# Splitting layer 0's sixteen input weight halves into high and low parts, with seven slots for the unsplit halves that follow

## The reference

```python
h = rms_norm(x, norm_g)
a_u, a_v, a_g, b_q, b_k, b_v, b_g, m_q, m_g = split_cols(h @ w_in, EVEN_SPLITS)   # w_in 1024 x 4096
y_a = chunked_sgu(gelu(a_u), gelu(a_v), ...) * silu(a_g)
q = rope(rms_norm(b_q.reshape(..., 8, 2, 32)));  k likewise       # 16 sub-heads of width 32
o_b = rms_norm(diff_attention(q, k, v, lam)) ; y_b = o_b * silu(b_g)
y_m = memory_attention(m_q, mem_n, m_wkv, ...) * silu(m_g)        # keys and values from mem
return x + concat([y_a, y_b, y_m]) @ w_out
```

## Time and profile before

| what | us |
|---|---|
| median of 3 runs (1028.76 to 1029.42) | 1029.19 |
| the profiled execution | 1031.47 |
| its span, first to last instruction | 1029.7 |
| PE busy in the span | 946.3 |
| DVE busy | 445.9 |
| POOL busy | 440.5 |
| ACT busy | 328.3 |
| mean granted TensorE clock | 0.961 of full speed |

### The profile page before, as it was taken

How to read it: one execution, slowest core, us unless ns; L and a number is a source line. 1 busy time by engine, 2 the same in 40 slices (tenths; PEclk the granted TensorE clock), 3 DMA queues, 4 the chain that set the end, 5 groups by cost and what they waited for, 6 DMA issues and landing times.

```text
span 1029.7 us, 14942 instructions
## 1 busy us (share of the span) xinstructions
PE 946.3 (92%) x5860; PEld 849.2 (82%) x5860; DVE 445.9 (43%) x948; ACT 328.3 (32%) x607; POOL 440.5 (43%) x561
## 2 busy tenths in 40 slices
PE   4999899999999897989898999889999898999995
PEld 4888788888888775768798998789898898998994
DVE  1453555511357799661498126701020434322133
ACT  2201343102000144331344475444020443443441
POOL 0040000100110100002399678898270398999992
PEclk9999989999999988889899999989999999999999
DMA  8443223243434400141164435353534155555551
GB/s 340 135 163 123 82 82 102 67 159 123 162 124 164 164 6 37 41 169 50 44 246 142 143 123 187 111 173 102 204 124 164 42 179 167 177 194 181 177 181 55
DMA packets 37637, 139.33 MB, mean 135 GB/s; under 512 B 4288, under 2 KB 4288, under 8 KB 37312
## 3 DMA queue, kind: packets, MB, share of 16 engines
q1 hardware_dynamic: 37424, 136.97, 39.0%
q10 hardware_dynamic: 144, 1.41, 0.3%
HBM read 137.32 MB, written 1.05 MB: 134 GB/s over the span
## 4 chain that ended last, share of the span: by engine, by line
PE 24%; POOL 22%; DVE 2%; ACT 1%; issue 1%; DVEq 0%; ACTq 0%; POOLq 0%
POOL w_lo L1993 22%; PE psum L488 7%; PE psum L489 6%; PE psum L490 5%; PE psum L491 5%; DVE y_lo L1378 1%; PE psum L552 1%; PE psum L543 0%; POOL rstd L2001 0%; ACT w_hi L1003 0%; DVE h_rows L1446 0%; DVE h_lo L1352 0%; DVE h_rows L1974 0%; ACT act_tmp L1064 0%; ACT h_hi L1029 0%
## 5 line engine op out<-in xcount | busy, mean ns | idle before, releaser
L1993 POOL TENSOR_TENSOR w_lo<-raw,w_hi 128x256 fp32r<-128x256 f32 x536 | 405.5, 798 | 127.9 <-ACT w_hi L1003 65.7
L488 PE MATMUL psum<-w_whole,h_whole 128*128 128x256 f32 (+1 forms) x960 | 227.8, 393 | 3.0 <-ACT h_whole L1041 2.2
L2001 POOL TENSOR_TENSOR rstd<-mean_sq,minus_half 128x2 f32<-128x2 f32 (+4 forms) x20 | 34.6, 1731 | 456.4 <-DVE mean_sq L1390 456.4
L489 PE MATMUL psum<-h_hi,w_hi 128*128 128x256 f32 x704 | 202.6, 288 | 12.6 <-POOL w_lo L1993 12.2
L488 PEld LDWEIGHTS psum<-w_whole,h_whole 128*128 128x128 f32 x960 | 183.4, 198 | 28.9 <-ACT h_whole L1041 2.6
L490 PE MATMUL psum<-h_lo,w_hi 128*128 128x256 f32 x704 | 201.1, 286 | 0.0
L491 PE MATMUL psum<-h_hi,w_lo 128*128 128x256 f32 x704 | 200.9, 285 | 0.0
L1003 ACT ACTIVATE w_hi<-raw 128x1024 fp32r<-128x1024 f32 x136 | 139.5, 1055 | 118.6 <-DMA raw<-in_blocks 78.5
L489 PEld LDWEIGHTS psum<-h_hi,w_hi 128*128 128x128 f32 x704 | 137.1, 195 | 14.8 <-issue 14.6
L490 PEld LDWEIGHTS psum<-h_lo,w_hi 128*128 128x128 f32 x704 | 137.1, 195 | 0.1
L491 PEld LDWEIGHTS psum<-h_hi,w_lo 128*128 128x128 f32 x704 | 137.1, 195 | 0.0
(11 more groups left out here) (268 smaller groups left out, 1307.6 us busy)
## 6 DMA issues: line engine op xcount, KB each, us to landing
raw<-in_blocks SPq DMA_DIRECT2D x136, 512.0 KB, 3.5
w_whole<-in_blocks SPq DMA_DIRECT2D x96, 512.0 KB, 4.3
w_late<-in_blocks SPq DMA_DIRECT2D x20, 512.0 KB, 4.4
early<-in_early SPq DMA_DIRECT2D x1, 1647.0 KB, 7.2
attention<-in_late ACTq DMA_DIRECT2D x1, 1380.0 KB, 7.8
rows<-in_mem SPq DMA_DIRECT2D x2, 512.0 KB, 3.5
x<-in_x SPq DMA_DIRECT2D x1, 1024.0 KB, 9.4
out_x<-h_rows SPq DMA_DIRECT2D x2, 512.0 KB, 2.6
```

Of the source, the lines that this page charges most:

```text
L488: return nc.tensor.matmul(out, lhs[0], rhs[0], start=start, stop=stop, skip_group_check=shared_bank)
L489: nc.tensor.matmul(out, lhs[0], rhs[0], start=start, stop=False, skip_group_check=shared_bank)
L1993: ins = nc.gpsimd.tensor_tensor(lo[:, at], full[:, at], hi[:, at].bitcast(F32), ALU.subtract)
L2001: rstd_ready.mark(nc.gpsimd.tensor_tensor(rstd[:, n % 2, 0:width], mean_sq[:, n % 2, 0:width], minus_half[:, 0:width], ALU.pow), name, pool)
```

## The change

Layer 0's sixteen halves move from `WHOLE` to the head of `HALVES` (`L0_SPLIT`): they are split by ACT and POOL and multiplied in three products. x0's left factor is split into `h_hi` and `h_lo`. `WHOLE` keeps 32 halves, in seven slots (`WHOLE_RING`) of one tensor `first`, whose ten blocks are: 0 `h_whole`, 1 `y_whole`, 2 to 7 the bytes of the three slots `w_hi`, `w_lo`, 8 `mem_t`, 9 free. SP issues `kv0`, then the 32 quarters of layer 0, and then all other whole halves, each once its block is free. `level()` keeps the lead within layer 0 until block 2 begins.

```diff
-WHOLE = (both_of(["kv0", "b_q", "b_k", "m_qg0", "b_v"] + L0_FILL) + out_halves(0)
+L0_SPLIT = both_of(["b_q", "b_k", "m_qg0", "b_v"] + L0_FILL)
+WHOLE = (both_of(["kv0"]) + out_halves(0)
          + both_of(["kv1", "d_q", "dkv1", "c_b", "c_a", "dkv2", "m_qg1", "cmp_w1", "c_g", "d_g"]) + out_halves(1))
-HALVES = (both_of(["x_lru0", ...
+HALVES = (L0_SPLIT + both_of(["x_lru0", ...
+MEM_BLOCK = 8
+WHOLE_RING = [9, 4, 5, 6, 7, 2, 3]
+WHOLE_BLOCK = [9, 0] + [WHOLE_RING[j % len(WHOLE_RING)] for j in range(len(WHOLE) - 2)]
...
+        def block_left(eng, block):
+            eng.wait_ge(*whole_done[max(j for j, b in enumerate(WHOLE_BLOCK) if b == block)])
+        def slot_left(eng, j, part):
+            if len(L0_SPLIT) <= j < len(L0_SPLIT) + SPLIT_SLOTS:
+                block_left(eng, 2 + 2 * (j % SPLIT_SLOTS) + part)
...
             def level():
-                return begun[0] if begun[0] else -LEAD
+                if begun[0] <= len(L0_SPLIT):
+                    return min(begun[0], len(L0_SPLIT) - LEAD) if begun[0] else -LEAD
+                return begun[0]
...
-            project("b_q", h_whole)
+            project("b_q", h_t)
...
+                if q == 2 * len(L0_SPLIT) - 1:
+                    for j in range(2, len(WHOLE)):
+                        load_whole(j)
...
             square_sums("x0", x)
+            split_to(2)
             copy_chunk("kv0", mkv[:, 0])
-            even_sources("x0_", h_whole[0], E("l0_norm"))
+            sources_hi("x0_", h_t, E("l0_norm"))
+            split_to(SPLIT_SLOTS)
...
-            split_to(LEAD)
+            split_to(len(L0_SPLIT) + LEAD)
             x_ready.wait(act, "x2")
...
-            odd_sources("x0_", h_whole[0], E("l0_norm"))
+            split_to(SPLIT_SLOTS)
+            sources_lo("x0_", h_t, E("l0_norm"))
```

More of the change, by code:

```diff
@@ L27 @@
 SPLIT_SLOTS = 3
-WHOLE_SLOTS = 2 * SPLIT_SLOTS - 1
 LEAD = 2
@@ L251, in build @@
         with ExitStack() as first_layers:
[L252 to L255, removed]
+            first = first_layers.enter_context(nc.sbuf_tensor("first", [P, 10, HALF], F32))
+            h_whole, y_whole, mem_t = ([first[:, b, :].rearrange("p (k s) -> p k s", k=KT)] for b in (0, 1, MEM_BLOCK))
         h_t = (sb("h_hi", [P, KT, S], F32R), sb("h_lo", [P, KT, S], F32R))
@@ L339, in build @@
         late_landed = [sem(f"late_landed{i}") for i in range(LATE_WHOLE_SLOTS)]
-        whole_landed = [sem(f"whole_landed{i}") for i in range(WHOLE_SLOTS)]
+        whole_landed = {b: sem(f"whole_landed{b}") for b in sorted(set(WHOLE_BLOCK))}
         w_hi_ready = sem("w_hi_ready")
@@ L398, in wait_half @@
             if half in whole_index:
-                turn, i = divmod(whole_index[half], WHOLE_SLOTS)
-                eng.wait_ge(whole_landed[i], 32 * (turn + 1))
+                j = whole_index[half]
+                eng.wait_ge(whole_landed[WHOLE_BLOCK[j]], 32 * (WHOLE_TURN[j] + 1))
             elif half in late_index:
@@ L414, in half_view @@
             if half in whole_index:
-                parts = [w_whole[:, whole_index[half] % WHOLE_SLOTS, :]]
+                parts = [first[:, WHOLE_BLOCK[whole_index[half]], :]]
             elif half in late_index:
@@ L642, in _ @@
             turned(pe, "x0_2", "x0_3")
-            project("b_q", h_whole)
+            project("b_q", h_t)
             normed.wait(pe, "mk0")
             turn_pair("mk0", lambda a, t: mkv[:, 0, t, a * P:(a + 1) * P])
-            project("b_k", h_whole)
+            project("b_k", h_t)
             normed.wait(pe, "q")
@@ L653, in _ @@
                 turn_pair(f"k{j}", lambda a, t: rows[:, t, 2048 + (2 * j + a) * P:2048 + (2 * j + a + 1) * P])
-            project("b_v", h_whole)
+            project("b_v", h_t)
             normed.wait(pe, "mq0")
@@ L686, in layer_units @@
                     pass
-            layer_units(0, UNITS0, 0, operands0, (s for name, half in FILL[0] for s in rows_piece(name, half, h_whole)))
+            layer_units(0, UNITS0, 0, operands0, (s for name, half in FILL[0] for s in rows_piece(name, half, h_t)))
             pe.wait_ge(ws_ready, 1)
@@ L958, in _, with load_whole @@
             sp.dma_start(positions[:, :], positions_d).then_inc(loaded["positions"], 16)
-            for j in range(len(WHOLE)):
-                if j >= WHOLE_SLOTS:
-                    sp.wait_ge(*whole_done[j - WHOLE_SLOTS])
+            def load_whole(j):
+                ahead, block = whole_ahead(j), WHOLE_BLOCK[j]
+                if ahead is not None:
+                    sp.wait_ge(*whole_done[ahead])
+                elif 2 <= block < MEM_BLOCK:
+                    last = max(i for i in range(len(L0_SPLIT)) if i % SPLIT_SLOTS == (block - 2) // 2)
+                    sp.wait_ge(*half_done[last])
                 for n in range(2):
-                    sp.dma_start(w_whole[:, j % WHOLE_SLOTS, n * QUARTER:(n + 1) * QUARTER],
-                                 blocks_d[2 * j + n]).then_inc(whole_landed[j % WHOLE_SLOTS], 16)
+                    sp.dma_start(first[:, block, n * QUARTER:(n + 1) * QUARTER],
+                                 blocks_d[2 * j + n]).then_inc(whole_landed[block], 16)
+            for j in range(2):
+                load_whole(j)
             def load_late(j):
@@ L968, in load_late @@
                     sp.wait_ge(*late_done[j - LATE_WHOLE_SLOTS])
+                elif j == 0:
+                    sp.wait_ge(*whole_done[whole_index[("kv1", 1)]])
+                else:
+                    block_left(sp, 9)
                 for n in range(2):
@@ L998, in split_to @@
                         act.wait_ge(*half_done[j - SPLIT_SLOTS])
-                    else:
-                        slot_left(act, 2 * j)
+                    slot_left(act, j, 0)
                     for q in (2 * j, 2 * j + 1):
```

15 lines of the change are left out of this document (9 added, 6 removed).

## The result

The changed kernel takes **1044.3 us** in the median of four runs (1041.85 to 1046.97), the kernel before 1028.97 in the four beside it: a ratio of 1.0148, 95% interval 1.0108 to 1.0188. Foretold were 1044, a range of 1033 to 1055, and 0.90 for slower. The profiled execution of the changed kernel is the quickest of the four: 1041.85, span 1040.1, which is 10.4 over the span before.

What follows compares the result with a forecast made beforehand. PE was taken to bound the attention, with a DVE and POOL chain just keeping pace in the front. Front +14.2, attention -6.5 and passage +6.7 gave +14.4 on the median 1029.2: 1043.6, said as 1044, range 1033 to 1055.

Steps and rivals of the forecast that it cites:

- x0's sources and `mk0`: Start of layer 0's front: splitting x0 on ACT and DVE +2.3 us, DVE's small steps up to `mk0`'s mean square +4.0.
- q's power: Layer 0's front: q's power on POOL starts at 61.1 us against 54.42, +6.7.
- Norm and rotation of q, and k's mean square: Layer 0's front, DVE beside POOL's halves 4 and 5: norm and rotation +4.0 us, then k's mean square +0.5.
- Norm and rotation of k: Layer 0's front, DVE beside POOL's halves 6 and 7: +4.0 us, ending at 94.2.
- `b_v`: Last products before attention: two split halves at 5.76 us plus about 1.5 for a fallen clock, against 13.98: -1.0.
- Front: Layer 0 up to attention's start: 109.7 us instead of 95.5, +14.2; bounds 0 (no port conflict) and +20.
- Attention: Layer 0's attention units: split products save up to 9.8 us, less ACT and DVE charges: -6.5; bounds -9.8 and about +1.
- Transfers and slots: Weight loads: same bytes, later loads hidden, and seven slots give nothing over five: 0.
- Passage: End of layer 1 into block 2: all copies wait for c3, x2's power starts at 506.3 against 499.62, +6.7 us.
- PE's saving wins: Rival, decided in the front: it costs under 3 us, so the kernel is faster or unchanged, 1026 to 1028; chance 0.10.
- POOL and ACT hold the attention: Rival: front at +20, attention gives nothing, passage +7: +27 us, 1056; chance 0.10.
- Full blocking: Rival: nine DVE norm and rotation steps each wait a whole 0.70 subtraction, 6.3 us not 4.0, twice: 1048 to 1049; chance 0.15.

Runs made afterwards that it cites:

- the widths above: The changed kernel with POOL's subtractions 512 columns wide instead of 256: 1046.1 us, ratio 1.0168 to the kernel before; with 128 columns: 1112.74 us, ratio 1.0816.
- the run with fills: The changed kernel with POOL's subtractions of halves 2 to 7 replaced by two zero fills each: median 1031.0 us, ratio 1.0029 to the kernel before.
- the second profile: Profile from running the changed kernel again, nothing altered (the second comparison): median 1042.47 us, ratio 1.0144 to the kernel before.

## Why the prediction was right

Sign, places and mechanism held. That the time came within 0.3 us of 1044 is luck: the three places that were summed gave +12.4 in the traces instead of +14.4, and 2 to 3 us that no trace places fill the gap. Step by step:

- *x0's sources and `mk0`* (+2.3 and +4.0): its power came at 50.17 against 50.6 foretold for its mean square. Held.
- *q's power* (+6.7): 59.51 - 54.42 = +5.1. Too large by 1.6: q's mean square was there at 59.4, not 61.0. `mk0`'s power came half a us earlier than charged, and the three tiny steps lost 0.4 us, not 1.6.
- *Norm and rotation of q, and k's mean square* (+4.0 and +0.5): k's power moved from 69.40 to 79.49, another +5.0. Too small by 0.5.
- *Norm and rotation of k* (+4.0): 8.46 against 4.14, +4.3. Held. The reason given for the size was half wrong. I read +0.4 for a 512-column step as a milder kind of hindrance; the widths above show one rule for all steps. Nine steps at +0.40 to +0.57 make the 4.3.
- *`b_v`* (-1.0, of which 1.5 lost to a fallen clock): from the end of k's rotation to the scores 15.8 us against 16.4, -0.65. With a clock of 1.00 the run with fills took 14.2, so the fallen clock (0.91 from 94.5 to 109 in the changed kernel's profile) cost 1.6. Held.
- *Front*: +13.8 against +14.2. The low bound of 0, for no conflict on the port, was sound too: with fills the first scores stand at 94.83.
- *Attention* (-6.5): -8.1. A pair of units takes 7.36, with 7.3 foretold. Mis-sized and misplaced is the charge for ACT, 2.8 us at four GELU halves: PE's waits for ACT grew from 4.1 to 6.4, so 2.3: 0.8 in the wait behind `a_v`'s norm, and 1.5 right after it, where two copies stand before an evacuation and no GELU does. The 0.5 charged for that norm on DVE isn't there; its first step takes 1.23, as alone. That leaves -9.8 + 2.3 = -7.5; the second profile has 134.6 for this stretch, -7.5, and the last 0.6 of the first profile isn't placed.
- *Transfers and slots* (0): held, by the run with five slots. PE waits for `first` from DRAM once before x2, 2.2 us for `kv0`, where it waited 1.9 before.
- *Passage* (+6.7, power about 12 behind c3): +6.7 and 12.2. Held, and shown by moving c3.
- *Layer 1* (0): -1.2, its source not shown, as said above.
- *Sum*: +14.4 foretold; the medians differ by 15.3 and, in the second comparison, by 14.7. The two profiles differ by 10.4 and 11.9 in their spans (the first run of the kernel before that was profiled lies 2.3 over its median, that of the changed one 2.5 under its own). The stretches of the front, attention and passage give +12.4. The 2 to 3 us between that and the medians aren't placed in any stretch; no run settled them.

Of the rivals, *PE's saving wins* fell by the front, at 13.8 where it needed under 3. *POOL and ACT hold the attention* fell by the pair of 7.36. *Full blocking* was right in its mechanism and wrong in its price: DVE waits for whole subtractions, but a step hides 0.12 to 0.28 of each, so that nine cost 4.3 and not 6.3.

## What to carry to other kernels

A change that saves PE's time and pays in GpSimd's is worth what the stage's own bound allows: here the same split lost 13.8 us where DVE and POOL formed the chain and won 7 to 8 where PE was the bound, so split the change along that line before giving it up. Beside a GpSimd instruction that reads SBUF, count a chain of DVE steps by their number times GpSimd's instruction length, not by their columns; and choose that length by who waits: here 512 columns won 4 to 5 us where POOL bounded and lost 11 where DVE waited, and 128 columns won nothing even there, since POOL then needs longer for the same half. After renumbering a ring of buffers, look up who frees the slot that the next stage's first write needs: one swapped pair of blocks was worth 9 us.

## What the runs showed of the hardware

DVE steps with a single input in SBUF lose nearly as much beside subtractions as those with two. Two of the changed kernel's timeline, the first beside POOL's half 2, the second once POOL is idle again (it ended half 2 at 44.44):

```profile
40.96 0.65 DVE L1493 TENSOR_SCALAR rope_tmp<-rope_tmp 128x128 f32<-128x128 f32 x1
...
45.09 0.23 DVE L1493 TENSOR_SCALAR rope_tmp<-rope_tmp 128x128 f32<-128x128 f32 x1
```

Beside fills they took 0.24 to 0.36. Not slowed by POOL are reductions (1024 columns at 1.22) and steps that read one operand from PSUM (512 columns at 0.69), beside subtractions and without them. POOL's own powers take 5.43 in every run, but DVE stood idle beside them, so whether they can be slowed isn't shown. And the hindrance goes both ways: a subtraction takes 0.89 beside DVE's norms and 0.69 alone.
